# Third modulation set summed on VectorE beside the last attention heads, q and k gains folded into tables, probabilities copied by VectorE

## What is computed

```
mod = silu(c) @ w_ada + b_ada          -> shift1, scale1, gate1, shift2, scale2, gate2
h1  = RMSNorm(x) * (1 + scale1) + shift1
u   = h1 @ w_in                        -> conv GLU (2048) | q | k | v (1024 each) | gates (2048)
conv = swish(LayerNorm(conv31(GLU))) @ w_conv_out
q, k = RMSNorm over 64, gain, rotation of the first 16 of 64
attn = (softmax(q1 k1) - lam * softmax(q2 k2)) v, RMSNorm per head, @ w_attn_out
x   = x + gate1 * ((sigmoid(g_c) * conv + sigmoid(g_a) * attn) @ w_o)
h2  = RMSNorm(x) * (1 + scale2) + shift2
x   = x + gate2 * MoE(h2)              (router, top 4 of 32, clamped SwiGLU, w_up, w_down)
```

## Time and profile before

| | us |
|---|---|
| median of three runs | 1286.7 |
| lowest and highest | 1286.41, 1288.59 |
| profiled execution, its own time | 1286.41 |
| its span, first to last instruction | 1284.6 |
| PE busy | 1080.6 (84%) |
| DVE busy | 404.4 (31%) |
| ACT busy | 219.0 (17%) |
| POOL busy | 51.7 (4%) |
| HBM read | 473.03 MB, 369 GB/s over the span |

### The profile page before, as it was taken

One profiled execution on the slowest core, in us unless ns is written; L12 is line 12 of the kernel. 1 busy time (PEld: TensorE's weight loads), 2 busy tenths in 40 slices (PEclk: granted clock), 3 DMA queues, 4 the chain that ended last, 5 costly groups with the idle time before them and its releaser, 6 DMA issues.

```text
span 1284.6 us, 23431 instructions
## 1 busy us (share of the span) xinstructions
PE 1080.6 (84%) x9958; PEld 528.3 (41%) x9958; DVE 404.4 (31%) x1129; ACT 219.0 (17%) x461; POOL 51.7 (4%) x91
## 2 busy tenths in 40 slices
PE   8999999899998566669998657968669696999975
PEld 5864458788433122224443212423224242444431
DVE  1388997631232111112222111212112121232221
ACT  1111124640121000002211001201002110122110
POOL 2000000355000000000000000000000000000000
PEclk9999999999999887889999888989889898999998
DMA  9998672256879999999999999999999999599997
GB/s 328 349 371 327 239 285 92 106 181 228 325 323 427 428 427 428 427 427 429 426 429 427 427 428 427 426 425 429 428 427 429 425 429 427 241 429 428 428 426 312
DMA packets 66084, 475.81 MB, mean 370 GB/s; under 512 B 6329, under 2 KB 19966, under 8 KB 39390
## 3 DMA queue, kind: packets, MB, share of 16 engines
q1 hardware_dynamic: 62100, 471.36, 89.2%
q0 software_dynamic: 816, 1.84, 0.5%
q10 hardware_dynamic: 3098, 1.56, 0.5%
HBM read 473.03 MB, written 1.05 MB: 369 GB/s over the span
## 4 chain that ended last, share of the span: by engine, by line
PE 49%; DMA 41%; SPq 5%; ACT 3%; DVE 1%; another core or an unknown queue 1%; issue 1%; ACTq 0%; DVEq 0%
DMA weights<-in_w_down 27%; PE bank L1556 14%; DMA weights<-in_w_up 13%; PE bank L1288 7%; PE bank L1584 7%; PE bank L1281 6%; SPq L462 4%; PE bank L1273 2%; PE bank L1426 2%; PE bank L1498 2%; PE bank L1224 2%; PE bank L1485 1%; PE bank L1194 1%; DMA weights<-in_w_ada 1%; PE bank L1505 1%
## 5 line engine op out<-in xcount | busy, mean ns | idle before, releaser
L1556 PE MATMUL bank<-weights,buf_d 128*32 128x512 f32 x3008 | 394.6, 671 | 141.6 <-DMA weights<-in_w_up 141.6
L1556 PEld LDWEIGHTS bank<-weights,buf_d 128*32 128x32 f32 x3008 | 96.9, 117 | 405.0 <-DMA weights<-in_w_up 211.5
L1584 PE MATMUL bank<-weights,buf_d 128*32 128x256 f32 x3008 | 177.6, 382 | 42.7 <-DMA weights<-in_w_down 39.9
L1165 DVE TENSOR_SCALAR u_conv<-bank 128x256 f32<-128x256 f32 x47 | 20.0, 425 | 467.5 <-PE bank L1556 467.5
L774 ACT ACTIVATE u_conv<-u_conv 128x256 f32<-128x256 f32 x47 | 19.6, 416 | 708.5 <-DVE u_conv L1165 708.5
L1584 PEld LDWEIGHTS bank<-weights,buf_d 128*32 128x32 f32 x3008 | 90.7, 110 | 115.5 <-DMA weights<-in_w_down 51.6
L864 DVE SCALAR_TENSOR_TENSOR weights<-u_conv,weights 128x256 f32<-128x256 f32 x240 | 97.8, 481 | 0.5
L1281 PE MATMUL bank<-weights,buf_d 128*128 128x512 f32 x192 | 82.9, 594 | 0.0
L1177 DVE TENSOR_TENSOR buf_d<-bank,u_conv 128x256 f32<-128x256 f32 x47 | 20.0, 425 | 180.1 <-PE bank L1584 180.1
L774 ACT ACT_TABLE_LOAD x47 | 60.3, 1283 | 1.4 <-issue 0.5
L1288 PE MATMUL bank<-buf_d,weights 128*128 128x256 f32 x256 | 58.6, 383 | 0.0
(11 more groups left out here) (274 smaller groups left out, 799.4 us busy)
## 6 DMA issues: line engine op xcount, KB each, us to landing
weights<-in_w_up SPq DMA_DIRECT2D x128, 2048.0 KB, 35.5
weights<-in_w_down SPq DMA_DIRECT2D x64, 2048.0 KB, 39.2
weights<-in_w_in SPq DMA_DIRECT2D x10, 2048.0 KB, 15.5
weights<-in_w_ada SPq DMA_DIRECT2D x8, 2048.0 KB, 19.3
weights<-in_w_ada SPq DMA_DIRECT2D x8, 1024.0 KB, 11.3
weights<-in_w_in SPq DMA_DIRECT2D x8, 512.0 KB, 10.1
weights<-in_w_in SPq DMA_DIRECT2D x4, 1024.0 KB, 13.1
weights<-in_w_conv_out SPq DMA_DIRECT2D x2, 2048.0 KB, 11.3
```

Source lines behind the costliest of these rows:

```text
L1556: ins = t.matmul(UP[SLOTS * g:SLOTS * g + SLOTS, :], xgT[:, r, SLOTS * j:SLOTS * j + SLOTS], up_group(w[:, r, :], g), start=False, stop=(j ...
L1584: ins = t.matmul(DOWN[rows, 0:T], actT[:, r, at:at + SLOTS], w[:, g, r, T * q:T * q + T], start=False, stop=(h == 1 and g == 1 and r == 1))
```

## The change

The third set of modulation rows leaves TensorE's path between k and v. Its four blocks move in SP's list from ahead of v to behind the gates' blocks. VectorE multiplies the weights by silu(c), held one value per partition, and adds them up in place: eight products (`mod_product`) of 2048 columns, one each in heads 5, 6 and 7 (`MOD_AT = 5`) and five behind the normalised o. TensorE then sums over the partitions with a matrix of ones (`sum_rows`: four matmuls) behind the third `conv_out`; `ada_row(1)`, the transposes (`turn_rows(1)`) and the scaling of the router's weights follow behind that. The bias of this set is loaded straight into the rows. POOL's twelve DMAs now wait for `ada_row(1)`, and the split of the first piece for `turn_rows(1)`.

The gains of q and k: for the 16 rotated channels they are folded into tables (`turns`, cosine and sine times gain, six small operations once); for the other 48 the product of both gains is a scale on ACT's copy of k. The rotation is two products of 128 columns and two sums of 64 per tile.

`keep_aT` moves from ACT, where it stood behind the exponentials, to VectorE, where it stands behind `srec`; in head 7, `keep_aT(7)` stands behind product 2. Some taps move to earlier stretches. `HEAD_SLOT` goes from place 3 to place 7 of `SLOT_ORDER`, and SP's wait for `ebias_ready` from ahead of chunk 3 to ahead of chunk 7. Four more small loads go out on ACT's queue at the start.

```diff
-SLOT_ORDER = (0, VALUE_SLOT, 1, HEAD_SLOT, 2, 3, CONV_SLOT, GATE_SLOT, 4, 5, SMALL_SLOT)
+SLOT_ORDER = (0, VALUE_SLOT, 1, 2, 3, CONV_SLOT, GATE_SLOT, HEAD_SLOT, 4, 5, SMALL_SLOT)
+MOD_AT = 5
...
-        ADA0[1] = len(blocks)
-        blocks += [ada_block(8 * NB, i) for i in range(4)]
         V0 = len(blocks)
...
         blocks += [block_of(w_in, NB * i) for i in range(10, 14)]
+        ADA0[1] = len(blocks)
+        blocks += [ada_block(8 * NB, i) for i in range(4)]
...
+            used[ADA0[0] + i] = (ada_done, i + 1)
+            used[ADA0[1] + i] = (mod_summed, 2 * i + 3)
...
-            sp.wait_ge(ebias_ready, 3 * PARTS)
-            load_chunk(0, 3)
             for i in range(2):
                 sp.wait_ge(*used[AOUT0 + i])
-                load_chunk(0, 4 + i)
+                load_chunk(0, 3 + i)
             full(sp, YA_USE + 3)
+            load_chunk(0, 5)
+            sp.wait_ge(mixed, 4)
             load_chunk(1, 0)
-            sp.wait_ge(mixed, 4)
+            sp.wait_ge(ebias_ready, 3 * PARTS)
             load_chunk(1, 1)
...
                 if piece == 0:
                     pool.wait_ge(swish_ready, KD)
+                    for gi in range(2):
+                        pool.wait_ge(bank_free[ADA_USE[gi] % 4], ADA_USE[gi] // 4 + 1)
...
                     pool.wait_ge(mod_ready, 16 * 12)
+                    for gi in range(2):
+                        pool.wait_ge(bank_full[M2T_USE[gi] % 4], M2T_USE[gi] // 4 + 1)
...
+            for i, w in enumerate((q_norm_g, k_norm_g)):
+                for half in range(2):
+                    load(col_rows[26 + i:27 + i, HD * half:HD * half + HD], w, in_cols)
...
+                ins = s.copy(dst, src) if i < 4 else s.activation(dst, src, ACT.Copy, scale=cols[:, 28:29])
...
-                if h:
-                    keep_aT(h - 1)
                 use = gate_use(h)
...
+            def mod_product(k):
+                w, seen = (blk(ADA0[1] + j // 2, 2)[:, j % 2, :] for j in (k, max(k - 1, 0)))
+                if k % 2 == 0:
+                    dve.wait_ge(blk_full[place(ADA0[1] + k // 2)], 16 * loads_before[ADA0[1] + k // 2])
+                if k:
+                    dve.wait_ge(mod_summed, k)
+                    ins = v.scalar_tensor_tensor(w, w, c_act[:, k, 0:1], seen, ALU.mult, ALU.add)
+                else:
+                    ins = v.tensor_scalar(w, w, c_act[:, 0, 0:1], None, ALU.mult)
+                ins.then_inc(mod_summed, 1)
...
-                step(v.tensor_tensor(dst, dst, qk_g[:, which, :].unsqueeze(1).to_broadcast([P, 8, HD]), ALU.mult))
...
+                for j in range(2):
+                    turn = turns[:, which, j, tt, :, :].rearrange("p h j -> p (h j)").unsqueeze(1).to_broadcast([P, 8, ROT])
+                    ins = v.tensor_tensor(rot[:, j, :, :], x, turn, ALU.mult)
+                step(ins)
+                for j in range(2):
+                    ins = v.tensor_tensor(dst[:, :, HALF * j:HALF * j + HALF], rot[:, 0, :, HALF * j:HALF * j + HALF],
+                                          rot[:, 1, :, HALF - HALF * j:ROT - HALF * j], ALU.add)
...
-            ada_row(1)
             conv(2, 17, TAPS)
...
                 if h:
-                    full(dve, aT_use(h - 1))
+                    keep_aT(h - 1)
...
+                if h >= MOD_AT:
+                    mod_product(h - MOD_AT)
+            keep_aT(HEADS - 1)
             keep_o(HEADS - 1)
...
+            for k in range(HEADS - MOD_AT, KD):
+                mod_product(k)
...
+            for i in range(3):
+                mix_conv(i)
+            ada_row(1)
+            mix_conv(3)
...
-            fill(pe, ADA_USE[1])
-            for i in range(4):
-                ada_rows(ADA_USE[1], ADA0[1], i)
...
+            def sum_rows():
+                use = ADA_USE[1]
+                fill(pe, use)
+                pe.wait_ge(mod_summed, KD)
+                total = blk(ADA0[1] + 3, 2)[:, 1, :]
+                for gi in range(4):
+                    ins = t.matmul(bank(use)[32 * gi:32 * gi + 32, :], ones[:, 0:32], total[:, NB * gi:NB * gi + NB],
+                                   start=True, stop=True)
+                ins.then_inc(bank_full[use % 4], 1)
+
+            turn_rows(0)
...
             for i in range(3):
                 conv_out(i)
+            sum_rows()
             pe.wait_ge(on_ready, 1)
...
             conv_out(3)
+            turn_rows(1)
```

More of the change, by code:

```diff
@@ L127, in build @@
         early = slot(GATE_SLOT)
-        ada_bias = early[:, 0:3 * NB].rearrange("p (g n) -> p g n", g=3)
+        ada_bias = early[:, 0:2 * NB].rearrange("p (g n) -> p g n", g=2)
         convw_rows = early[:, 4 * NB:4 * NB + 2 * P].rearrange("p (a c) -> p a c", a=2)
@@ L344, in build @@
         order += [("ada", 0)] + [("qk", i) for i in range(8)]
-        order += [("ada", 1)] + [("v", i) for i in range(4)] + [("mod2T", 0), ("mod2T", 1)] + [("qkT", i) for i in range(8)]
+        order += [("v", i) for i in range(4)] + [("mod2T", 0)] + [("qkT", i) for i in range(8)]
         for h in range(HEADS + 1):
@@ L354, in build @@
                 order += [("var", 0)]
-        order += [("y_conv", i) for i in range(3)] + [("oT", i) for i in range(4)] + [("y_conv", 3)]
+        order += [("y_conv", i) for i in range(3)] + [("ada", 1)]
+        order += [("oT", i) for i in range(4)] + [("y_conv", 3), ("mod2T", 1)]
         order += [(name, i) for name in ("y_attn", "w_o") for i in range(4)]
@@ L829, in _ @@
                     step(v.tensor_scalar(cols[:, 25:26], cols[:, 24:25], SUBLN, None, ALU.mult))
+                    step(v.tensor_tensor(cols[:, 28:29], cols[:, 26:27], cols[:, 27:28], ALU.mult))
+                    for half in range(2):
+                        step(v.memset(cols[HD * half:HD * half + ROT, 28:29], 1.0))
             def ada_row(gi):
                 use = ADA_USE[gi]
-                dve.wait_ge(in_rows2, 64)
+                dve.wait_ge(in_rows2, 128)
                 full(dve, use)
-                v.tensor_tensor(modrow2[:, gi, :], bank(use)[:, :], ada_bias[:, 1 + gi, :], ALU.add).then_inc(bank_free[use % 4], 1)
+                bias = modrow2[:, 1, :] if gi else ada_bias[:, 1, :]
+                v.tensor_tensor(modrow2[:, gi, :], bank(use)[:, :], bias, ALU.add).then_inc(bank_free[use % 4], 1)
+            def mod_product(k):
[8 more added lines that the diff above has]
+                ins.then_inc(mod_summed, 1)
             def glu_tile(k):
@@ L953, in _, with keep_aT @@
             v.tensor_copy(by_chunk[:, 0, :, :, :], columns(0, 2)).then_inc(bank_free[M2T_USE[0] % 4], 1)
-            full(dve, M2T_USE[1])
-            v.scalar_tensor_tensor(by_chunk[:, 1, :, :, :], columns(1, 0), 1.0, gain, ALU.add, ALU.mult).then_inc(
-                bank_free[M2T_USE[1] % 4], 1)
-            conv(3, 11, 19)
+            conv(3, 11, 21)
+            def keep_aT(h):
+                use = aT_use(h)
+                full(dve, use)
+                v.tensor_copy(aT[:], bank(use)[:, 0:384]).then_inc(bank_free[use % 4], 1)
             def keep_o(h):
@@ L1309, in _, with turn_rows @@
                 value(i)
-            for gi in range(2):
+            def turn_rows(gi):
                 use = M2T_USE[gi]
```

76 lines of the change are left out of this document (39 added, 37 removed).

## The result

| | before | after |
|---|---|---|
| median, us | 1286.9 (8 runs) | 1290.8 (8 runs, 1289.94 to 1291.98) |
| ratio, 95% interval | | 1.0029, 1.0020 to 1.0038 |
| profiled execution, its span | 1286.41, 1284.6 | 1291.5, 1289.7 |

The change makes the kernel 0.3% slower: 4.0 us by the medians, 5.1 us by the spans of the two profiled executions. The forecast was 1285.3 us.

What follows compares the result with a forecast made beforehand. The end was the routing's finish, on TensorE's run up to 363.6 us, plus a fixed stream of 182 chunks. -6.95 + 0.1 + 1.75 + 2.8 + 0.44 + 0.45 = -1.4 us gave 1285.3 us, range 1283.0 to 1288.5.

Steps and rivals of the forecast that it cites:

- B: Rival: TensorE's clock falls in the wait at attend(7), price 1.7 us, 1287.0 us in all; chance 0.11.
- C: Rival: POOL's expert biases, ready at 339 us, become the bound past 346.7; at 353, 1291.6 us; chance 0.07.
- four signs of being wrong: attend(0) waits over 1 us; clock below 1.00 before 355; POOL wait past 347; routing-to-end gap changes over 1 us.
- `attend(0)`: At the start of the heads: it starts 6.95 us sooner, between 6.2 and 7.4.
- `attend(1)`: In the heads: margin nil for the copy of aT(1) on VectorE, +0.1 us.
- waits at `attend(3)`, (4), (5): In the heads: three closed loops each grow by 0.58 us for the copy on VectorE, +1.75 us.
- from `attend(6)` to `attend(7)`: Last head: product 2 has no cover ahead of the copy of aT(7), 4.2 us against 1.4, +2.8 us.
- `sum_rows`: Behind the heads: four added matmuls, 4 x 7.0/64, +0.44 us.
- Rival A: In the heads: the stalls do not grow, sum -4.2, 1282.5 us; chance 0.14.
- VectorE, not TensorE, sets the pace here: Ahead of the heads: VectorE takes 7.76 us per step, against 6.89 us for a projection on TensorE.
- D: Rival: the start is not covered, w_ada's first rows are handled late, 1 to 2 us, 1286.8 us; chance 0.05.
- E: Rival: the third set's blocks arrive late for product 4 or 6; no size given; chance 0.01.

Runs made afterwards that it cites:

- the kernel with one product later: The changed kernel with product 2 moved from head 7 to behind the normalised o, so six products follow there: 1287.74 us, ratio 1.0003.
- The chunks held back: The changed kernel with SyncE waiting for POOL's twelve small gate-row DMAs to land before it issues chunk 0: 1290.06 us, ratio 1.0023.
- three buffers alone: The changed kernel with all nine expert-bias loads issued at once at 251 us into three parts of HEAD_SLOT, products unchanged: 1289.26 us, ratio 1.0020.

## Why the prediction was wrong

Two terms that the forecast put at nothing came true together. I had them as rivals, B with a chance of 0.11 and C with 0.07, each alone. B is the clock: the sum lets TensorE keep its clock through the long wait at `attend(7)`. C is the biases: the sum lets POOL finish in time for the stream. Of my four signs of being wrong three showed: a granted clock below 1.00 (0.50 at `attend(7)`), SyncE's wait for POOL past 347 us (353.2), and the time from the first unit to the end, changed by 2.3 us. So the end hangs on the routing only with the condition that I had put beside it, that no chunk comes late. The sum against the two profiled executions; the rows of the heads go from start to start of the named matmuls:

| step of the prediction | predicted, us | measured, us |
|---|---|---|
| `attend(0)` | -6.95 | -7.44 |
| `attend(1)` | +0.1 | (204.24 - 194.32) - (211.05 - 201.76) = +0.63 |
| waits at `attend(3)`, (4), (5) | +1.75 | 2.12 + 1.74 + 1.68 - (4.3 - 0.91) = +2.15 |
| from `attend(6)` to `attend(7)` | +2.8 | (262.80 - 257.90) - (264.49 - 262.43) = +2.84 |
| rest of the heads | 0 | some +0.1 |
| clock in `attend(7)` | rival B | (264.21 - 262.80) - (265.24 - 264.49) = +0.66 |
| clock in the three `conv_out` | rival B, 1.7 | 23.06 - 20.89 = +2.17 |
| `sum_rows` | +0.44 | +1.00 |
| `turn_rows(1)` | +0.45 | +0.47 |
| oT | 0 | some +0.15 |
| biases against the stream | rival C | +2.3 |
| sum | -1.4 | +5.1 |

**The clock (rival B).** The step that failed is the term of nothing for TensorE's clock behind a wait of 4.2 us: it cost 2.17 us in `conv_out` and 0.66 in `attend(7)`. The forecast made a wait that was longer than any in before, and no row of before showed the clock up behind one like it. In before the clock stayed at 1.00 behind waits of 1.4 us and fell behind the sparse routing; here it fell behind 0.46 and 3.01 us with three transposes between them. Nor are the heads safe: the same wait of 2.1 us at `attend(3)` left the clock up in after and not in the kernel with one product later. So 0.11 was too little for B. The price by the routing's row, 1.7 us, was 0.5 to 1.1 too low. The rule of the Trainium skill (TensorE: Matmul & The Clock Gate, part 1), that the array falls to half clock after idling and returns once busy, is what the trace shows. There the granted clock and two lengths of the same matmul, 0.64 and 0.39 us, stand for it.

**The biases (rival C).** The mechanism and its point of decision, as the rival had them, were right: a moved wait, three chunks queued behind it, 14.7 us for them. The ready time was not. From the first split to the end I had 41.7 us and it was 40.5. The twelve DMAs were issued at 290.05 and not at 285, and 2.8 of these 5.0 us are B's, through the later end of `conv_out`. And from their first issue to the first split it was 22.6 us, where I took 12.4 from a stretch in which DMA was half idle. That is the term mis-sized: 10.2 us, and the stretch where the price was read had another load than the one where it was used. The chunks held back show it. 339 + 5.0 + 10.2 - 1.2 = 353 us. The decision then fell at 365.5 - 14.7 = 350.8.

**`sum_rows`.** 4 x 7.0/64 counted 64 rows as 64 matmuls. They are 32: every fp32 matmul has two records (four of `sum_rows` show as x8). 4 x 7.0/32 = 0.88, measured 1.00.

**The heads.** The three loops grew by 0.72 us each, not 0.58; the copy and its handovers on VectorE were that much dearer. At `attend(1)`, where the margin was put at nil with 0.1 us lost, it was 0.63 us. Rival A's reason against itself held. The loop at `attend(7)` was sized well: +2.84 us for +2.8, and from the end of `attend(6)`, 258.42 + 0.39, to 262.80 it is 4.0 us, predicted 4.2, with product 2 in its place. `pa(7)`, which I had 0.6 us before TensorE wants it, came 0.46 us after, inside the same wait.

**VectorE's pace.** "VectorE, not TensorE, sets the pace here" is wrong for the kernel before: the tables alone brought it nothing. It holds once `ada_rows` is gone: without the tables TensorE then waits 6.01 us for VectorE. With the tables TensorE starts `attend(0)` without a wait, so the measured 7.44 us is TensorE's own 7.45 and not VectorE's 6.95.

**What was right.** The gain at `attend(0)`, the order at `attend(7)`, the covered start (TensorE still waits 0.99 us for w_ada, so not D), and the third set's blocks in time (not E). The port pair, weighed there at 0.2 us for product 1, cost it about 0.05 (2.39 against 2.34 us), but the probabilities just ahead of it 0.90 instead of 0.35 us.

**What stays open.** Why the clock falls behind a wait of 2.1 us in one execution and not in another, and why it came back sooner in some (`conv_out` 21.84 us with three buffers alone, behind the same wait of 3.01 us, so that some of that kernel's 1.6 us is the clock's), was not tried. The routing is no steadier: its longest wait in after is 0.7 us, as in before, yet in after the clock stayed at 1.00 behind it and the first up stage took 6.87 us, not 8.57. At the end of the run this 1.7 us is not seen, since the chunks and not TensorE set the time there.

## What to carry to other kernels

Price a new wait on TensorE with what it does to the clock behind it, and ask of each product that is to run "in the shade" what is queued behind it on its engine: one product later was worth 3.1 us. A long wait can cost twice, once as a wait and once more behind it. A small transfer that is moved behind the start of a bulk stream costs what it costs in that stream, so issue it before, into its own buffer. And take from a change only the parts that pay: removing the work from TensorE and shortening VectorE's step belong together, while moving the copy to VectorE gave 2.75 us away.

## What was not expected of the hardware

VectorE and POOL slow each other in both directions: a POOL operation of 1024 columns takes 4.04 instead of 2.12 us beside VectorE's products, these take 3.12 instead of 2.41 us each, and a VectorE operation of two columns 1.67 instead of 0.23 us beside a split. Twelve small DMAs of POOL's queue take 16.73 us to land, from the end of their issue, while SyncE's 2 MB chunks stream, and 4.29 us without them. In the kernel with one product later it was 9.23 us with the chunks. The Trainium skill (DMA: Bandwidth & Descriptors, Queues, rings and completion order) has each DMA engine take turns between the queues that have work for it, a packet at a time; by that alone I would not have expected a factor of four, and no run here separates its parts.
